# Paged cache loads of a hybrid S5 and MLA decoder step: two tokens to a partition on 64 partitions

## The chip, the cores and the metric

The kernel runs on one core of one Trainium2 chip. The metric is the device time of one execution in microseconds, the median over runs. All data are 32-bit floats.

## What is computed

One layer of a decoder, for a prompt of 512 tokens (with 16 learned meta tokens ahead of it) and for 8 samples that decode one token each. An input projection feeds an S5 state-space group and a latent attention group (MLA, 8 heads); both are gated, concatenated and projected back. What the change touches is the attention of the 8 samples over their cached past, 2048 tokens in 16 pages of 128 for each sample:

```python
def mla_sample_attn(q_abs, q_pe, c_new, kpe_new, c_pool, kpe_pool, page_table, w_uv):
    c_past = c_pool[page_table].reshape(dbs, -1, KV_LORA)        # KV_LORA = 512
    kpe_past = kpe_pool[page_table].reshape(dbs, -1, QK_ROPE)    # QK_ROPE = 64
    s_past = (jnp.einsum('bqhr,bkr->bhqk', q_abs, c_past)
              + jnp.einsum('bqhe,bke->bhqk', q_pe, kpe_past)) * SOFTMAX_SCALE
    ...
    w = jax.nn.softmax(jnp.concatenate([s_past, s_new], axis=-1), axis=-1)
    o_lat = (jnp.einsum('bhqk,bkr->bqhr', w[..., :n_past], c_past)
             + jnp.einsum('bhqk,bkr->bqhr', w[..., n_past:], c_new))
```

A page of cache_ckv is 128 x 512 floats (256 KB), one of cache_kpe 128 x 64 floats (32 KB). Which pages a sample has stands in a page table that is read at run time.

## The kernel before, in words

The program is written out engine by engine, with semaphores between them. Its stages in order of time are: normalising and transposing the input, the input projection, the S5 scan with its gate, the query, key and value projections, the attention of prompt and samples together, and the output projection with the final norm. The projections run on TensorE (PE) as three matmuls for each product, of high and low parts.

The attention stage is a loop over 32 steps n (`N_TILES`, four for each of 8 heads), unrolled on every engine. At each step the engines do one 128-query tile of the prompt's attention, and beside it one group of pages of a sample: 32 groups, four pages each, four groups for each sample.

- **Slots.** Seven slots (`RING`, line 412) hold a group each: `ckv[s]` is [128 partitions, 4, 512] and `kpe[s]` [128, 4, 64]; the second index j is the page of the group, and the partition is the token in the page.
- **Loads.** `load_pages` (lines 455 to 465) reads page numbers from the table into registers, waits until the slot's last user on PE is done (`opv_done`), and issues two DMAs for each page, one of cache_ckv (line 464) and one of cache_kpe (line 465). The first seven groups are loaded whole, one by SyncE's queue (SP, line 653) and six by GpSimd's (POOL, lines 814 to 826), ahead of the loop. Of each of the other 25 groups, SP loads pages 0 and 1 (lines 671 to 673) and POOL pages 2 and 3 (lines 827 and 828). On SP these loads stand in a written order between the loads of the prompt's heads: `hraw` (queries and keys, lines 618 to 625, of which line 624 loads rotary queries twice, once to partitions 0 to 63 and once to 64 to 127), `vraw` (line 629), `za` (line 633), and small stores to `u_d` (line 685).
- **Order.** `freed_at` (line 433) gives the step at which a slot is freed. Two groups are freed together, every two steps or so, so loads come in bursts of two groups. Each DMA adds 16 to a semaphore of its slot and queue; `loaded_counts` (line 450) gives the counts to wait for, 64 for each round of two pages on each queue.
- **Users.** VectorE (DVE) waits for a group (line 1790) and transposes it in 32 x 32 blocks, in two halves of two pages (`turn_pages`, line 1793), and its rotary keys (`turn_rotary`, line 1797). PE computes scores of two groups at once (`page_scores`, lines 2350 and 2354), DVE and ScalarE (ACT) do the maximum and the exponential, and at the steps of `freed_at` PE weighs the pages with their probabilities straight from `ckv[s][:, j, :]` (`weigh_pages`, line 2378), which frees the slot. The scores take keys as they come: each place (partition, j) of a group is one key, in ckv and in kpe alike.

Of the kernel before, what the change touches and what calls it, by code (L numbers as in the profile page):

```python
# [13 lines left out]
ds = bass.ds  # L14
# [49 lines left out]
def build(nc, d):  # L64
# [4 lines left out]
    def at(name, offset, shape, dt=F32):  # L69

        assert base + offset + math.prod(shape[1:]) * 4 <= 229344, name
        return nc.alloc_sbuf_tensor_at(name, shape, dt, offset=base + offset)

    with es:
        def sem(name):
            return es.enter_context(nc.semaphore(name))
# [102 lines left out]
        ckv = [at(f"ckv{i}", a, [P, 4, KV_LORA]) for i, a in enumerate(SLOT_AT)]  # L179
        kpe = [at(f"kpe{i}", a + 8192, [P, 4, QK_ROPE]) for i, a in enumerate(SLOT_AT)]  # L180
# [151 lines left out]
        page_loaded = [[sem(f"page_loaded_{q}{s}") for s in range(7)] for q in ("pool", "sp")]  # L332
# [96 lines left out]
        def pages_freed(i):  # L429

            return i + 1
# [23 lines left out]
        def load_pages(eng, i, halves, by_sync):  # L455

            pages = [eng.value_load(ptab[0:1, 4 * i + j:4 * i + j + 1], min_val=0, max_val=d["cache_ckv"].shape[1] - 1)
                     for half in halves for j in (2 * half, 2 * half + 1)]
            if i >= RING:
                eng.wait_ge(opv_done, pages_freed(i - RING))  # L460
            s = i % RING
            for at_j, page in enumerate(pages):
                half, j = halves[at_j // 2], 2 * halves[at_j // 2] + at_j % 2
                eng.dma_start(ckv[s][:, j, :], d["cache_ckv"][0, ds(page, 1)].rearrange("a k r -> (a k) r")).then_inc(page_loaded[by_sync][s], 16)  # L464
                eng.dma_start(kpe[s][:, j, :], d["cache_kpe"][0, ds(page, 1)].rearrange("a k r -> (a k) r")).then_inc(page_loaded[by_sync][s], 16)

        MX, NMS, SMS = 0, 8, 16

# [3 lines left out]
        def _(sp):  # L472
# [178 lines left out]
            sp.wait_ge(table_loaded, 16)  # L651
            sp.wait_ge(v_ready, 10)
            load_pages(sp, BY_SYNC, (0, 1), 1)
            for u in range(2):
                sp.wait_ge(v_stored[u], 16 * 5)
# [9 lines left out]
            for n in range(N_TILES):  # L665
                h = n // 4 + 1
                if n % 4 == 1 and h + 1 < N_HEADS:
                    sp.wait_ge(head_lo_done, h + 1)
                    load_raw(h + 1)
                    load_rotary(h + 1)  # L670
                for i in range(RING, N_GROUPS_OF_PAGES):
                    if freed_at(i - RING) == n:
                        load_pages(sp, i, (0,), 1)
                if n % 4 == 0 and n and h < N_HEADS:
                    sp.wait_ge(pv_done, h - 1)
                    load_v(h)
                    sp.wait_ge(o_gated, h - 1)
                    load_za(h)
                if n % 4 == 3 and 0 <= n // 4 - 1 < N_SAMPLE - 2:
                    s = n // 4 - 1  # L680
                    sp.wait_ge(o_copied, s + 1)
                    if s:
                        sp.wait_ge(rows_stored, 64 * s)
                    for j in range(4):
                        sp.dma_start(u_d[s * P + 32 * j:s * P + 32 * j + N_HEADS, 0:KV_LORA], osb[32 * j:32 * j + N_HEADS, s % 2, :]
                                     ).then_inc(rows_stored, 16)
# [50 lines left out]
        def _(pool):  # L737
# [76 lines left out]
            for i in (4, 5):  # L814
                load_pages(pool, i, (0, 1), 0)
# [1744 lines left out]
```

## Time and profile before

| | |
|---|---|
| median of 3 runs | 1157.97 us (1156.71 to 1161.84) |
| the profiled execution | 1155.58 us |
| its span | 1153.9 us |
| mean granted TensorE clock | 0.964 of full speed |
| PE busy | 1045.1 us, 91% |
| DVE busy | 609.7 us, 53% |
| ACT busy | 378.0 us, 33% |
| POOL busy | 170.6 us, 15% |
| bytes moved by DMA | 170.93 MB, 148 GB/s over the span |
| attention stage | about 723 to 928 us |

All durations below are from the one profiled execution. The times of an engine are busy times; its idle times are attributed to what released it. A DMA packet is a piece that one of the 16 DMA engines moves in one go; the share of a queue is the time its packets took, over 16 engines times the window. "Landing" is from the issue of a DMA to its completion.

### The profile page before, as it was taken

How to read it: one execution, taken by the hardware profiler on the slowest of the kernel's cores; microseconds unless marked ns; L12 is line 12 of the kernel's file. 1: busy time of each engine (PE TensorE's matmuls, PEld its weight loads, DVE VectorE, ACT ScalarE, POOL GpSimd, SP SyncE). 2: the span in 40 equal slices, each digit the busy share in tenths (PEclk: the TensorE clock that was granted, in tenths of full speed). 3: DMA queues.
4: the chain of work that ended last, by engine and by line, in shares of the span. 5: the costliest groups of instructions: out<-in, count | busy, mean ns of one | idle time of the engine just before them, and what ended most of it. 6: DMA issues, size and time to landing. Idle time of an engine off the chain costs nothing.

```text
span 1153.9 us, 26835 instructions
## 1 busy us (share of the span) xinstructions
PE 1045.1 (91%) x10642; PEld 964.7 (84%) x10642; DVE 609.7 (53%) x1253; ACT 378.0 (33%) x774; POOL 170.6 (15%) x257
## 2 busy tenths in 40 slices
PE   3899999999999999998899989678777789999995
PEld 2899999999999999997799977555545549999995
DVE  4366454451688821495765355767668542332432
ACT  6321112212233222154542222444545412332433
POOL 3002310000320000103504500123333100000000
PEclk9899999999999999999899989798999889999998
DMA  9446743223344443237456845567787786223213
GB/s 281 102 139 115 167 118 94 71 69 93 114 119 129 115 131 92 73 93 226 124 158 183 257 167 161 157 214 242 251 251 255 235 203 215 74 80 102 73 37 148
DMA packets 202059, 170.93 MB, mean 148 GB/s; under 512 B 37755, under 2 KB 166246, under 8 KB 200134
## 3 DMA queue, kind: packets, MB, share of 16 engines
q1 hardware_dynamic: 179078, 120.75, 37.5%
q0 software_dynamic: 11392, 28.52, 8.0%
q10 hardware_dynamic: 11496, 20.36, 4.8%
q8 instruction: 65, 1.06, 0.4%
q14 instruction: 28, 0.23, 0.1%
HBM read 141.93 MB, written 25.31 MB: 145 GB/s over the span
## 4 chain that ended last, share of the span: by engine, by line
PE 72%; DMA 9%; DVE 6%; issue 5%; ACT 4%; SPq 3%; POOLq 0%; ACTq 0%; POOL 0%; DVEq 0%
PE gemm L2065 12%; PE gemm L2066 12%; PE gemm L2067 12%; PE gemm L2420 5%; PE gemm L2422 5%; PE gemm L2421 5%; DMA kpe<-cache_kpe 4%; PE misc L2141 2%; PE misc L2336 2%; PE misc L2151 1%; PE misc L2092 1%; DMA w_raw<-w_glu 1%; DMA w_raw<-w_in 1%; PE gemm L2350 1%; DMA osr<-u_d 1%
## 5 line engine op out<-in xcount | busy, mean ns | idle before, releaser
L2065 PE MATMUL gemm<-xh,w_hi 128*128 128x260 f32 (+2 forms) x1056 | 302.3, 286 | 0.3 <-DVE w_lo L1333 0.3
L2066 PE MATMUL gemm<-xl,w_hi 128*128 128x260 f32 (+2 forms) x1056 | 300.7, 285 | 0.0
L2067 PE MATMUL gemm<-xh,w_lo 128*128 128x260 f32 (+2 forms) x1056 | 299.9, 284 | 0.0
L1333 DVE TENSOR_TENSOR w_lo<-w_raw,w_hi 128x2048 fp32r<-128x2048 f32 (+3 forms) x63 | 109.6, 1739 | 225.3 <-ACT w_hi L857 221.7
L857 ACT ACTIVATE w_hi<-w_raw 128x2048 fp32r<-128x2048 f32 (+3 forms) x63 | 90.7, 1439 | 337.2 <-PE gemm L2067 281.7
L2065 PEld LDWEIGHTS gemm<-xh,w_hi 128*128 128x128 f32 x1056 | 198.8, 188 | 1.2 <-DVE w_lo L1333 0.5
L2067 PEld LDWEIGHTS gemm<-xh,w_lo 128*128 128x128 f32 x1056 | 199.1, 189 | 0.0
L2066 PEld LDWEIGHTS gemm<-xl,w_hi 128*128 128x128 f32 x1056 | 198.9, 188 | 0.0
L2420 PE MATMUL gemm<-comb_hi,w_hi 128*128 128x260 f32 x512 | 147.7, 289 | 1.2 <-DVE comb_lo L1945 1.1
L2421 PE MATMUL gemm<-comb_lo,w_hi 128*128 128x260 f32 x512 | 145.3, 284 | 0.0
L2422 PE MATMUL gemm<-comb_hi,w_lo 128*128 128x260 f32 x512 | 145.3, 284 | 0.0
L2420 PEld LDWEIGHTS gemm<-comb_hi,w_hi 128*128 128x128 f32 x512 | 97.1, 190 | 4.0 <-issue 3.2
L2421 PEld LDWEIGHTS gemm<-comb_lo,w_hi 128*128 128x128 f32 x512 | 97.4, 190 | 0.0
L2422 PEld LDWEIGHTS gemm<-comb_hi,w_lo 128*128 128x128 f32 x512 | 97.3, 190 | 0.0
L1793 DVE STREAM_TRANSPOSE ct<-ckv 128x1024 f32<-128x1024 f32 x64 | 79.2, 1238 | 33.9 <-DMA kpe<-cache_kpe 33.6
L1934 DVE TENSOR_TENSOR yt<-yt,misc 128x512 f32 (+1 forms) x14 | 9.6, 687 | 98.5 <-PE misc L2481 98.5
L464 POOL DMA_DIRECT2D ckv<-cache_ckv x74 | 40.0, 541 | 144.1 <-PE gemm L2378 102.4
L1249 ACT ACTIVATE yb<-gemm 128x260 f32<-128x260 f32 x28 | 9.3, 385 | 106.2 <-PE gemm L2422 106.2
L1888 DVE TENSOR_TENSOR w_lo<-w_raw,w_hi 128x2048 fp32r<-128x2048 f32 x16 | 36.7, 2292 | 13.3 <-ACT w_hi L1237 13.2
L2164 PE MATMUL gemm<-ys_hi,w_hi 128*128 128x260 f32 x128 | 38.2, 298 | 5.1 <-DVE sig L1633 4.4
L2350 PE MATMUL gemm<-ct,qx 128*32 128x64 f32 x2048 | 38.9, 243 | 2.8 <-issue 2.8
L2065 PE MATMUL gemm<-qn_hi,w_hi 128*128 128x260 f32 x144 | 40.8, 283 | 0.5 <-DVE ev L1694 0.5
(383 smaller groups left out, 1990.2 us busy)
## 6 DMA issues: line engine op xcount, KB each, us to landing
w_raw<-w_in SPq DMA_DIRECT2D x35, 1024.0 KB, 6.3
ckv<-cache_ckv POOLq DMA_DIRECT2D x74, 256.0 KB, 4.3
w_raw<-w_out SPq DMA_DIRECT2D x16, 1024.0 KB, 5.8
ckv<-cache_ckv SPq DMA_DIRECT2D x54, 256.0 KB, 4.3
z_d<-ev ACTq DMA_DIRECT2D x16, 260.0 KB, 2.0
w_raw<-w_glu SPq DMA_DIRECT2D x8, 512.0 KB, 4.3
yt<-x_prompt SPq DMA_DIRECT2D x4, 1024.0 KB
o_y_p<-yt SPq DMA_DIRECT2D x4, 1024.0 KB
```

Of the source, the lines that this page charges most:

```text
L464: eng.dma_start(ckv[s][:, j, :], d["cache_ckv"][0, ds(page, 1)].rearrange("a k r -> (a k) r")).then_inc(page_loaded[by_sync][s], 16)
L857: act.activation(w_hi[:, slot, 0:width], w_raw[:, slot, 0:width], ACT.Copy).then_inc(w_hi_ready, 1)
L1333: dve.tensor_tensor(w_lo[:, slot, 0:width], w_raw[:, slot, 0:width], w_hi[:, slot, 0:width].bitcast(F32), ALU.subtract).then_inc(w_lo_read ...
L1793: dve.transpose(out=ct[:, n % 3, first:last].rearrange("p x r -> p (x r)"), in_=ckv[n % RING][:, first:last].rearrange("p x r -> p (x r)"))
L2065: pe.matmul(acc, a, xa, start=k == 0, stop=False)
L2066: pe.matmul(acc, a, xb, start=False, stop=False)
L2067: last = pe.matmul(acc, b, xa, start=False, stop=k == k_tiles - 1)
L2164: pe.matmul(acc, a, xa, start=k == 0, stop=False)
L2350: pe.matmul(SC[32 * j:32 * j + 32, c0:c0 + 64].rearrange("p (g t) -> p g t", g=2), qx[:, s % 2, r, :], ct[:, buffers, j, r * 32:(r + 1) * ...
L2420: pe.matmul(acc, a, comb_hi[:, k, c], start=k == 0, stop=False)
L2421: pe.matmul(acc, a, comb_lo[:, k, c], start=False, stop=False)
L2422: last = pe.matmul(acc, b, comb_hi[:, k, c], start=False, stop=k == KD - 1)
```

## The change

Each page goes to 64 partitions in place of 128, and each partition takes two consecutive tokens, which lie side by side in the pool and in the slot: 4096 contiguous bytes of cache_ckv and 512 of cache_kpe, where there were 2048 and 256. Pages 0 and 1 of a group share the columns j = 0 and 1 of the slot, page 0 on partitions 0 to 63 and page 1 on 64 to 127; pages 2 and 3 share j = 2 and 3 in the same way. The slots, semaphores, counts, queues and all that uses the pages stay as they are.

```diff
@@ -461,8 +461,11 @@
             s = i % RING
             for at_j, page in enumerate(pages):
                 half, j = halves[at_j // 2], 2 * halves[at_j // 2] + at_j % 2
-                eng.dma_start(ckv[s][:, j, :], d["cache_ckv"][0, ds(page, 1)].rearrange("a k r -> (a k) r")).then_inc(page_loaded[by_sync][s], 16)
-                eng.dma_start(kpe[s][:, j, :], d["cache_kpe"][0, ds(page, 1)].rearrange("a k r -> (a k) r")).then_inc(page_loaded[by_sync][s], 16)
+                rows, cols = slice(64 * (j % 2), 64 * (j % 2) + 64), slice(j - j % 2, j - j % 2 + 2)
+                eng.dma_start(ckv[s][rows, cols, :].rearrange("p t r -> p (t r)"), d["cache_ckv"][0, ds(page, 1)].rearrange("a (k t) r -> (a k) (t r)", t=2)
+                              ).then_inc(page_loaded[by_sync][s], 16)
+                eng.dma_start(kpe[s][rows, cols, :].rearrange("p t r -> p (t r)"), d["cache_kpe"][0, ds(page, 1)].rearrange("a (k t) r -> (a k) (t r)", t=2)
+                              ).then_inc(page_loaded[by_sync][s], 16)
 
         MX, NMS, SMS = 0, 8, 16
```

## Rows read from the trace of the kernel before

**Rows 1.** Chain of waits that ended last, 723 to 928 us: shares by line

```profile
by line: DMA kpe<-cache_kpe 22.3%; issue 15.7%; PE misc L2336 8.7%; PE gemm L2350 6.1%; PE gemm L2378 5.1%; DVE ct L1793 4.2%; SPq L465 3.6%; SPq L464 3.6%; PE misc L2315 2.7%; SPq L457 2.6%; SPq L624 2.0%; ACT prob L1170 1.7%; ACT hh L1067
```

**Rows 2.** List of waits, 715 to 935 us: total, times, longest

```profile
POOL ckv L464 <- PE gemm L2378: 102.4, 13, 27.7
...
DVE ct L1793 <- DMA kpe<-cache_kpe: 33.6, 18, 5.4
...
DVE mxt L1806 <- PE gemm L2354: 15.0, 6, 6.1
...
SPq L464 <- PE gemm L2378: 41.6, 8, 12.1
```

**Rows 3.** Timeline of SP's queue, one burst: start, duration

```profile
829.10 0.38 SPq L464 DMA_DIRECT2D ckv<-cache_ckv  x1
...
830.72 0.33 SPq L465 DMA_DIRECT2D kpe<-cache_kpe  x1
...
832.90 1.31 SPq L465 DMA_DIRECT2D kpe<-cache_kpe  x1
```

**Rows 4.** Timeline of POOL, the same burst

```profile
829.57 0.54 POOL L464 DMA_DIRECT2D ckv<-cache_ckv  x1 [10.00 <-PE gemm L2378]
...
831.62 0.54 POOL L465 DMA_DIRECT2D kpe<-cache_kpe  x1
```

**Rows 5.** Timeline of DVE, the same burst: idle time before, releaser

```profile
836.46 1.25 DVE L1793 STREAM_TRANSPOSE ct<-ckv 128x1024 f32<-128x1024 f32 x1 [1.86 <-DMA kpe<-cache_kpe]
```

**Rows 6.** Busy time by stretch; the last three: clock, DMA share, GB/s

```profile
820.00:845.00 25.00, 20.70 (x484) 14.43 (x476) 18.43 (x42) 11.45 (x35) 8.39 (x16) 0.98 0.78 249
```

**Rows 7.** DMA queues, 804 to 826 us (q1 is SP's, q0 POOL's)

```profile
DMA packets 4421, 6.18 MB, mean 281 GB/s; under 512 B 1680, under 2 KB 2208, under 8 KB 4416
...
q1 hardware_dynamic: 3520, 3.75, 56.6%
q0 software_dynamic: 896, 2.36, 31.8%
```

**Rows 8.** DMA queues, 739.0 to 739.5 us: 128 partitions, rows of 2 KB

```profile
q1 hardware_dynamic: 102, 0.19, 100.5%
```

**Rows 9.** DMA queues, 627 to 628 us (256 B), then 1000 to 1012 us (512 B)

```profile
q1 hardware_dynamic: 988, 0.25, 109.8%
...
q1 hardware_dynamic: 2064, 1.05, 31.1%
```

**Rows 10.** DMA queues, 740.1 to 740.7 us: two loads to 64 partitions each

```profile
DMA packets 110, 0.18 MB, mean 305 GB/s; under 512 B 21, under 2 KB 21, under 8 KB 110
...
q1 hardware_dynamic: 110, 0.18, 95.2%
```

**Rows 11.** Issue durations by line, ns: minimum, median, maximum, first and last start

```profile
L464 POOL DMA_DIRECT2D ckv<-cache_ckv x74: 537/537/709, 627.6 to 902.6; - x74
...
L464 SPq DMA_DIRECT2D ckv<-cache_ckv x54: 332/333/377, 722.6 to 902.1; - x54
...
L809 POOL DMA_DIRECT2D rp<-lat_d x2: 543/561/579, 626.5 to 627.1; - x2
...
L789 POOL DMA_DIRECT2D latq<-lat_d x1: 855/855/855, 522.4 to 522.4; - x1
...
L624 SPq DMA_DIRECT2D hraw<-qp_d x16: 458/550/1423, 702.8 to 863.2; - x16
```

**Rows 12.** DMA queues, 811 to 823 us, inside a burst

```profile
DMA packets 2787, 3.93 MB, mean 327 GB/s; under 512 B 869, under 2 KB 1397, under 8 KB 2785
```

**Rows 13.** Landing: the page's issues, 638 to 648 us, and cache_ckv's minimum

```profile
ckv<-cache_ckv POOLq DMA_DIRECT2D x74, 256.0 KB, 4.3
...
kpe<-cache_kpe SPq DMA_DIRECT2D x54, 32.0 KB, 5.0
...
ckv<-cache_ckv POOLq DMA_DIRECT2D x6, 256.0 KB, 3.3
...
DMA to landing us min/median/max: 2.5/4.3/6.6
```

## The prediction, made before the change was run

> **What bounds the kernel now.** I read the page first: PE is busy 91% of the span, and the paged attention is a stretch of about 205 us in the middle. Then I asked for the chain of waits over that stretch [rows 1]. The reader is to see that the largest share of it, 22.3% of 205 us or 45.7 us, is the flight of a page load, and that the rest is spread thin over PE, DVE, ACT and the queues. So here, unlike in the projections before and after, loads end waits. The list of waits says who waits [rows 2]: the DVE transposes of the pages lose 33.6 us in 18 waits to a cache_kpe load, which is the last DMA of a group on its queue. In the other direction POOL waits 102.4 us and SP 41.6 us until PE has weighed a group and its slot is free. That is the loop: PE frees a slot, both queues issue, the pages land, DVE transposes, PE scores and weighs.
>
> One turn of it in the timelines: SP issues its two pages of a group from 829.10 to 831.05 and has the next group under issue at 832.90 [rows 3]; POOL issues its two from 829.57 on, the last at 831.62 [rows 4]; DVE, which had to wait, starts on that group at 836.46 [rows 5]. So the group took 7.4 us from the first issue, of which 4.8 us lie after the last issue. Between 820 and 845 us the 16 DMA engines are busy 78% of the time at 249 GB/s, with the bursts near full and gaps between them [rows 6]. Both the throughput inside a burst and the latency at its end count.
>
> **What a page load costs in the DMA engines, and what the change makes of it.** A page is 262 KB of cache_ckv and 33 KB of cache_kpe. In the burst of 804 to 826 us SP and POOL load eight pages each. SP's queue shows 3520 packets, POOL's 896 [rows 7]. POOL's divide as 16 completions for each of 16 DMAs (256) and 640 data packets, 80 a page: with 2.36 MB that is 64 packets of 4 KB and 16 of 2 KB. So POOL's queue already joins two 2 KB rows into one packet. SP's are one for each contiguous row: of the 1680 packets under 512 B 256 are POOL's completions, and the other 1424 are 8 x 128 rows of cache_kpe and 400 completions of SP's.
>
> Prices of a packet, as the share of 16 engines times the window over the count:
> - 2 KB: 100.5% of 8 us over 102 packets is 79 ns [rows 8].
> - 256 B: 109.8% of 16 us over 988 is 17.8 ns; 512 B: 31.1% of 192 us over 2064 is 28.9 ns [rows 9].
> - A completion: in a window with 21 of them and 89 of 2 KB, 9.14 us less 89 x 79 ns leaves about 100 ns each [rows 10].
> - 4 KB: POOL's 31.8% of 352 us is 111.9 us; less 256 x 0.1 and 128 x 0.079 us there remain 76.2 us for 512 packets, 149 ns [rows 7].
>
> SP's page before: 128 x 79 ns + 128 x 17.8 ns = 10.1 + 2.3 = 12.4 us of engine time; after: 64 x 149 ns + 64 x 28.9 ns = 9.5 + 1.8 = 11.4 us. With 3.2 us for 32 completions, which stay, the saving is 1.0 of 15.6 us, that is 0.066 us of all 16 engines. POOL's page: the same 64 packets of 4 KB and, with four partitions of 512 B for an engine where there were eight of 256 B, the same 16 of 2 KB. Saving none.
>
> **Issue.** As many DMAs are issued as before: 54 + 54 on SP, 74 + 74 on POOL, with the same table reads before them. SP takes 333 ns for each, and POOL 537 ns [rows 11]. On POOL 64-row transfers took 561 ns, and one of 768 rows 855 ns, so halving the rows lies between -0.03 and +0.03 us for a DMA; I take 0. On SP the nearest 64-row row is 550 ns [rows 11], but that one has a strided source; the ends are 0 and +0.2 us for each of four DMAs of a group, and the first page's DMAs overlap with the flight, so +0.4 us for 18 waits, +7 us, is the upper end. I take 0, since a page's own source is contiguous. SP's occasional issue of 1.3 us (at 832.90 [rows 3]) is backpressure; half the descriptors may end it, which I leave at nothing to -1 us a period, about -6 us over the six periods of some 25 us, value 0: the engines are busy then.
>
> **Consumers.** The DVE transposes and PE's weighing read the same shapes of the same tiles; keys only change places, in ckv and kpe alike, and a softmax sum doesn't see their order. Counts of the semaphores stay (16 for each DMA), so no wait is added. So I cost them at nothing, and no cover is needed.
>
> **The sum.** A group holds two SP pages: -0.13 us. A burst is two groups, so its second group gains up to -0.26 us. Over 18 waits this is -2.4 to -4.7 us; I take -3. The profiled execution took 1155.6 us (span 1153.9) and so would give 1152.6; the median of the runs shown is 2.4 us above it, and on that scale I say 1155. The whole wait of 33.6 us is the lower end of what can be won, and it cannot be reached: the fastest landing of a page still takes 2.5 us [rows 13]. What is late next is PE's last score matmul, for which DVE waits 15 us in the stretch already [rows 2].
>
> **A place where row and rule part.** The two halves of the rotary queries are 64-partition loads on SP, one to partitions 0 to 63, then one to 64 to 127, just as this change does with pages. While they land, 740.1 to 740.7 us, the queue moves 305 GB/s, and with completions taken off, the packets cost what those of a 128-partition load cost [rows 8, 10]. By this row a half costs nothing, and it is why I take no penalty. It is 262 KB long, and partly both halves at once, so it does not exclude one. The Trainium skill ("SBUF — State Buffer", Door 1: The DMA port swizzle) speaks against the change: partitions 0 to 63 reach 8 of 16 ports, it gives 196 GB/s for 64 partitions and 328 for 128, and its next section says that two loads, one on each half, gain only 6%. Here 305 GB/s disagrees. By its asymptote of about 218 GB/s a page would take an estimated 1.35 us in place of 0.90, and if 18 waits pay that once, the time would be near 1166, if for all four pages, near 1190.
>
> **Rivals.**
> 1. Half the partitions, half the rate. Place: the start and the end of each burst, where one page of one queue flies alone, or all of it, if SP's and POOL's pages fall on the same half at the same time (both queues start with partitions 0 to 63). Price: at 327 GB/s, the rate of a burst [rows 12], a page of 295 KB takes 0.90 us, at half of it 1.80 us. One page for each of 18 waits: +16 us, 1174. All four pages of each: a period of 25 us, busy 19.5 us now, gets 16 x 0.9 = 14.4 us more, and so exceeds 25 us by 9; six periods make +54 us, 1212. For it: no row shows a transfer as long as a page to one half, from two queues at once. Against: rows 10; and POOL starts 0.5 us after SP, so that the queues may be on different halves. It decides as soon as an engine's 4 KB packet takes clearly over 149 ns. Slower than before.
> 2. The load's latency falls by more than its engine time. Landing takes 4.3 us (cache_ckv) and 5.0 (cache_kpe on SP) in the median, but 3.3 us in a stretch where POOL's loads are nearly alone [rows 13]. If SP's many small packets and its blocked issues make up this difference, 18 waits lose about 1 us each: -18 us, 1140. For it: POOL's packets, which are large, wait in the same engines as SP's 256 B ones, in turns. Against: the engine time saved is 6%.
> 3. The change does nothing: POOL's half of the pages sees the same packets, and on SP 2 KB packets run at nearly the rate of 4 KB ones (79 x 2 against 149 ns). Time 1158.
>
> **How the numbers follow.** Small gain, as summed: 0.42 (range 1150 to 1161). Rival 1: 0.25 for one page a wait, 0.10 for more. Rival 2: 0.20. Rival 3: 0.03. A measurement of this kernel tells about 0.5%, 5.8 us, from no change. Faster by over that: rival 2 and 0.09 of the first case, 0.29. Within: 0.33 + 0.03 = 0.36. Slower: 0.35. Cases of both signs hold most of the chance, so the range is wide: from 1143, which leaves out about half of rival 2, to 1179, which holds the lighter form of rival 1 and leaves out the heavy one.
>
> **What would show it.** Right: SP's queue shows 128 data packets a page in place of 256, POOL's keeps 80 data packets a page; 4 KB packets near 149 ns on both; DVE's wait for cache_kpe falls to about 30 us; DVE, PE and issue durations unchanged. Rival 1: packet time well over 149 ns, the rate in a burst under 300 GB/s, DVE's wait over 45 us, DMA share in the stretch towards 1. Rival 2: landing near 3.5 us and the wait near 15. The forecast is wrong if that wait moves by more than 6 us either way.

## The result and the profile after

| | before | after |
|---|---|---|
| median of the runs, us | 1157.34 (4 runs, 1154.73 to 1161.84) | 1215.89 (4 runs, 1211.19 to 1217.57) |
| ratio after to before, 95% interval | | 1.0482 [1.0453, 1.0512] |
| span of the profiled execution, us | 1153.9 | 1212.5 |
| mean granted clock | 0.964 | 0.944 |

The change costs 58 us. The prediction, 1155 in a range of 1143 to 1179, is wrong.

Where the time went, first by stretches of the kernel after: length, busy time of PE, weight load, DVE, ACT and POOL, then clock, DMA share and GB/s.

```profile
600.00:720.00 120.00, 109.39 (x767) 100.69 (x766) 55.86 (x99) 26.69 (x41) 29.91 (x49) 0.94 0.66 174
720.00:985.00 265.00, 182.13 (x3274) 121.78 (x3276) 148.35 (x322) 99.94 (x293) 58.39 (x109) 0.84 0.80 183
985.00:1212.00 227.00, 208.45 (x1745) 198.26 (x1737) 73.10 (x114) 69.20 (x208) 0.65 (x1) 0.95 0.40 117
```

The same stretches of the kernel before:

```profile
600.00:720.00 120.00, 115.20 (x828) 104.37 (x827) 59.93 (x106) 30.72 (x45) 30.41 (x49) 0.97 0.61 190
720.00:928.00 208.00, 160.19 (x3239) 107.93 (x3241) 145.13 (x316) 97.29 (x289) 60.60 (x109) 0.90 0.73 227
928.00:1153.00 225.00, 207.27 (x1733) 197.98 (x1725) 72.06 (x114) 68.73 (x207) 0.00 (x0) 0.96 0.40 117
```

The last stretch, after the attention, is as long as before (227 against 225 us). The attention has the same work (DVE 148 against 145 us busy) in 265 us in place of 208. The DMA engines are busier (0.80 against 0.73) and move less (183 against 227 GB/s). So each byte costs more engine time; there is no lack of requests. Already from 600 to 720 us, when POOL loads the first pages beside weights, the rate falls from 190 to 174 GB/s, and PE is busy 5.8 us less in that stretch. PE's granted clock falls in the attention from 0.90 to 0.84 of full speed, and less in the stretches around it (0.97 to 0.94 and 0.96 to 0.95). PE waits more there; I read the fall as a consequence of the waits, which no run isolates. For the same matmuls PE is busy 182 in place of 160 us. Most of that is not on the chain of waits below: PE's lines there hold some 42 us, where they held 46.

The waits of the kernel after, 715 to 990 us (total, times, longest), answer to [rows 2]:

```profile
POOL ckv L465 <- PE gemm L2381: 131.9, 12, 30.2
DVE ct L1796 <- DMA kpe<-cache_kpe: 81.1, 20, 8.7
...
DVE mxt L1809 <- PE gemm L2357: 14.0, 4, 6.4
```

DVE's wait for a page has grown from 33.6 us in 18 to 81.1 us in 20: +47.5 us, beside a loss of 58. What was named as late next, the wait for PE's score matmul, has hardly moved. The chain that ended last, 723 to 985 us, by line, and its longest pieces (start, us), answers to [rows 1]:

```profile
by line: DMA kpe<-cache_kpe 32.7%; issue 14.9%; SPq L465 5.9%; PE gemm L2381 5.2%; SPq L467 4.7%; PE misc L2339 4.7%; PE gemm L2353 4.3%; SPq L457 2.7%; SPq L633 2.4%; PE misc L2318 1.7%; SPq L627 1.6%; DVE ct L1796 1.5%; POOLq L74 1.0%; SP
...
777.33 13.15 DMA kpe<-cache_kpe
...
810.02 12.43 DMA kpe<-cache_kpe
...
842.19 12.63 DMA kpe<-cache_kpe
...
874.24 13.14 DMA kpe<-cache_kpe
...
907.14 13.64 DMA kpe<-cache_kpe
```

By these shares the flights of pages on the chain hold 85.7 us (32.7% of 262) where they held 45.7, and SP's page issues 27.8 where they held 14.8. Once a period of the attention (32.4 us, four groups) there is one flight of 12.4 to 13.6 us. It belongs to the first group that SP issues behind the loads of the prompt's next head, as its timeline shows for the third of them (842.19):

```profile
837.65 1.11 SPq L627 DMA_DIRECT2D hraw<-qp_d  x2
...
842.19 0.47 SPq L467 DMA_DIRECT2D kpe<-cache_kpe  x1
```

The packets of that group wait behind those of the head's loads on SP's queue: by the packet records it moves mostly the head's rows from 840 to 845 us, and the pages' 4 KB packets from there to 855. POOL's pages share the engines from 843 on. Before, this place had the longest flight too, and it was shorter:

```profile
866.75 8.93 DMA kpe<-cache_kpe
```

The period, start to start of those flights, is 32.4 us (777.33 to 907.14 in four), where the prediction worked with 25. Five such periods at +7.4 us make 37 us, and the rest of the 58 lies at the edges of the attention. Some 8 us of it are lost before the loop has begun: SP issues its first page at 730.3 us in place of 722.6.

The queues, 750 to 990 us, which hold 50 of POOL's pages in either kernel (packets, MB, share of 16 engines): before, then after.

```profile
q1 hardware_dynamic: 37534, 38.74, 54.5%
q0 software_dynamic: 5600, 14.75, 18.5%
```

```profile
q1 hardware_dynamic: 20739, 28.92, 51.1%
q0 software_dynamic: 5600, 14.75, 28.0%
```

POOL's queue moves the same bytes in the same number of packets, 112 a page with completions, for half as much engine time again: 18.5% of 3840 us over 50 pages was 14.2 us a page, 28.0% is 21.5. In the trace's packet records of the same window (size and duration of each packet), POOL's 3200 packets of 4 KB rise from 193 to 291 ns in the mean (medians 162 and 302). In the microsecond from 798 to 799 POOL's page flies alone:

```profile
DMA packets 63, 0.22 MB, mean 221 GB/s; under 512 B 9, under 2 KB 9, under 8 KB 63
...
q0 software_dynamic: 54, 0.22, 104.7%
q1 hardware_dynamic: 9, 0.00, 1.0%
```

104.7% of 16 us over 54 packets is 310 ns for 4 KB, and the rate is 221 GB/s with all engines busy. The nine other packets are completions, and they took 0.16 us together, 18 ns each. In the packet records before, a completion takes 9 to 10 ns. The prediction had priced it at about 100, and so had put too much of POOL's time down to completions: its 149 ns for a packet of 4 KB [rows 7] were 191 in that burst, with the median at 169. The count of packets came out as predicted. Their price rose to one and a half times in the mean, and to about twice the median of before when a page flies alone. Landing and issues answer to [rows 13] and [rows 11]:

```profile
ckv<-cache_ckv POOLq DMA_DIRECT2D x74, 256.0 KB, 7.3
...
ckv<-cache_ckv SPq DMA_DIRECT2D x54, 256.0 KB, 7.9
```

```profile
L465 POOL DMA_DIRECT2D ckv<-cache_ckv x74: 516/521/531, 625.8 to 958.2; - x74
...
L465 SPq DMA_DIRECT2D ckv<-cache_ckv x54: 468/469/1333, 730.3 to 957.9; - x54
```

A page lands in 7.3 us where it took 4.3. Besides, SP needs 469 ns for an issue in place of 333. That is a second candidate.

### The profile page after: what moved, and what is told of

Same layout as the page of the kernel before. It is cut to its first block, busy times and chain, and to the rows that moved or that the text cites. A ratio compares the mean times of both kernels' runs of the same rounds, so it can differ in the third digit from the quotient of the medians.

```text
span 1212.5 us, 26835 instructions
## 1 busy us (share of the span) xinstructions
PE 1062.9 (88%) x10642; PEld 975.8 (80%) x10642; DVE 607.4 (50%) x1253; ACT 377.9 (31%) x774; POOL 168.3 (14%) x257
## 2 busy tenths in 40 slices
DMA packets 195147, 170.93 MB, mean 141 GB/s; under 512 B 30843, under 2 KB 162790, under 8 KB 193222
## 4 chain that ended last, share of the span: by engine, by line
PE 68%; DMA 12%; DVE 5%; SPq 5%; issue 5%; ACT 3%; POOLq 0%; ACTq 0%; DVEq 0%; POOL 0%
PE gemm L2068 12%; PE gemm L2069 11%; PE gemm L2070 11%; DMA kpe<-cache_kpe 7%; PE gemm L2423 5%; PE gemm L2425 5%; PE gemm L2424 5%; DMA w_raw<-w_uk 2%; PE misc L2144 2%; SPq L465 1%; PE misc L2154 1%; PE gemm L2381 1%; PE misc L2095 1%; DMA w_raw<-w_glu 1%; DMA w_raw<-w_in 1%
## 5 line engine op out<-in xcount | busy, mean ns | idle before, releaser
L1796 DVE STREAM_TRANSPOSE ct<-ckv 128x1024 f32<-128x1024 f32 x64 | 79.2, 1238 | 81.4 <-DMA kpe<-cache_kpe 81.1
L2353 PEld LDWEIGHTS gemm<-ct,qx 128*32 128x32 f32 x2048 | 37.5, 131 | 7.1 <-issue 6.7
```

The lines of the kernel that those rows point to most:

```text
L1796: dve.transpose(out=ct[:, n % 3, first:last].rearrange("p x r -> p (x r)"), in_=ckv[n % RING][:, first:last].rearrange("p x r -> p (x r)"))
L2353: pe.matmul(SC[32 * j:32 * j + 32, c0:c0 + 64].rearrange("p (g t) -> p g t", g=2), qx[:, s % 2, r, :], ct[:, buffers, j, r * 32:(r + 1) * ...
```

## The experiments

The main theory: the 64 contiguous partitions are the cause; what goes into one half of the partitions is limited to about 210 GB/s. Against this theory stood the long packet itself, both queues on the same half at the same time, SP's dearer issue, and engines that reach one half slowly. The diffs are against the changed kernel where nothing else is said.

**Every second partition in place of a half.** Same packets, same 64 rows, other partitions.

```diff
-                rows, cols = slice(64 * (j % 2), 64 * (j % 2) + 64), slice(j - j % 2, j - j % 2 + 2)
+                rows, cols = slice(j % 2, P, 2), slice(j - j % 2, j - j % 2 + 2)
```

> A page still goes to 64 partitions with two tokens each, but to every second partition of the 128 (page j on partitions j mod 2, j mod 2 + 2, ...) in place of one half. Theory 1, the half: what the changed kernel lost, it lost because the 64 partitions of a page lie in one half of the SBUF, into which only some 220 GB/s go (its bursts run flat at 200 to 240 GB/s, before 270 to 370). Then this layout is as fast as before or a little faster, 1150 to 1158 us, bursts at 300 GB/s or more, 4 KB packets near 149 ns. Theory 2, the long packet: 4 KB written into a single partition take 310 ns in place of two times 79. Then this one is as slow as the changed kernel, 1210 to 1220 us, with packets near 310 ns. Theory 3, the queue: an issue on SP takes 469 ns in place of 333 with this access pattern, four times a group; then nothing changes against the changed kernel either, 1216 us, at whatever rate of the bursts.

Measured: 1165.51 against 1159.97 us, ratio 1.0059 [1.0035, 1.0082], a little slower than the 1150 to 1158 that the theory gave. Landing of cache_ckv (POOL, then SP, as in all that follows) is 4.4 and 4.3 us, DVE's wait 42.6 us in 16. POOL's pages are back at the old engine time (750 to 990 us), and inside a burst, 798 to 802 us, the rate is that of before or more:

```profile
q0 software_dynamic: 5600, 14.75, 18.6%
```

```profile
DMA packets 708, 1.48 MB, mean 370 GB/s; under 512 B 163, under 2 KB 351, under 8 KB 708
```

One line brings the loss from 4.82% to 0.59%, with the long packets left in. The cause of most of it is which partitions the rows go to.

**The half without the long packet.** 64 contiguous partitions, but rows of 2 KB: tokens k and k + 64 share a partition.

```diff
-                eng.dma_start(ckv[s][rows, cols, :].rearrange("p t r -> p (t r)"), d["cache_ckv"][0, ds(page, 1)].rearrange("a (k t) r -> (a k) (t r)", t=2)
+                eng.dma_start(ckv[s][rows, cols, :], d["cache_ckv"][0, ds(page, 1)].rearrange("a (t k) r -> (a k) t r", t=2)
...
```

> The changed kernel with 2 KB packets: page j on the same 64 partitions of one half, but token k and token k + 64 of the page go to partition k, so every run of contiguous bytes is one token (2048 bytes of cache_ckv, 256 of cache_kpe). Theory 1, the half: as slow as the changed kernel, 1205 to 1225 us, bursts at 200 to 240 GB/s. Theory 2, the long packet: back near the kernel before, 1150 to 1165 us. Theory 3, the queue: depends on the issue time that the profile then shows; at 469 ns like the changed kernel 1216 us, at 333 ns 1157 us.

Measured: 1217.87 against 1159.97 us, 1.05 [1.0468, 1.0533]; landing 7.0 and 7.5 us. The half costs all of it even with rows of 2 KB. SP's page packets are of 2 KB here; POOL's are as many as before (5600 in the window), so its queue still joins two rows, and only their destination is split. Issues are dearer still (604 ns on POOL, 605 on SP), and that too hardly shows.

**Opposite halves on the two queues.** SP begins with partitions 0 to 63 and POOL with 64 to 127.

```diff
-                rows, cols = slice(64 * (j % 2), 64 * (j % 2) + 64), slice(j - j % 2, j - j % 2 + 2)
+                side = (j + j // 2) % 2
+                rows, cols = slice(64 * side, 64 * side + 64), slice(j - j % 2, j - j % 2 + 2)
```

> The changed kernel, but pages 2 and 3 of a group, which POOL loads, change halves: page 2 goes to partitions 64 to 127, page 3 to 0 to 63. SP still begins with 0 to 63. So at any time the two queues tend to fill different halves. Theory 1, the half: most of the loss comes back, since both halves fill at once: 1155 to 1180 us, bursts mostly over 280 GB/s. Theory 2, the long packet, and theory 3, the queue: no change against the changed kernel, 1210 to 1220 us.

Measured: 1211.04 us, 1.0451 [1.0422, 1.048]; landing 7.0 and 7.0 us, DVE's wait 68.9 us in 20. A miss: I had expected most of the loss to go. The two queues being on one half together is not the main thing.

**A quarter for each page.** Page j lies on partitions 32j to 32j + 31, in rows of 8 KB.

```diff
-                rows, cols = slice(64 * (j % 2), 64 * (j % 2) + 64), slice(j - j % 2, j - j % 2 + 2)
+                rows = slice(32 * j, 32 * j + 32)
...
+                eng.dma_start(ckv[s][rows, :, :].rearrange("p t r -> p (t r)"), d["cache_ckv"][0, ds(page, 1)].rearrange("a (k t) r -> (a k) (t r)", t=4)
...
```

> Each page goes to 32 partitions with four tokens each (8192 contiguous bytes of cache_ckv): page j on partitions 32 j to 32 j + 31. SP's pages 0 and 1 both lie in the first half, POOL's 2 and 3 both in the second. Theory 1, the half: each queue has a half of its own, some 220 GB/s each, together up to 440, if a quarter takes as much as a half: 1150 to 1170 us. If instead the rate goes with the number of partitions of a page, 32 are half as fast again, and it is slower than the changed kernel: over 1260 us. Theory 2, the long packet: packets of 8 KB into one partition take 620 ns, and it stays at 1210 to 1220 us or above.

Measured: 1213.13 us, 1.0469 [1.0447, 1.0491]; landing 7.7 and 6.7 us. A miss as well: SP's pages now lie in the lower half and POOL's in the upper, throughout, and it is no better than the change. SP's issue fell to 316 ns here, so with an issue as cheap as in the kernel before the loss stays.

**Every fourth partition.** As the quarters, but spread, again 8 KB rows. The diff is against the quarters.

```diff
-                rows = slice(32 * j, 32 * j + 32)
+                rows = slice(j, P, 4)
```

> Each page on 32 partitions with four tokens each, but on every fourth of the 128 (page j on j, j + 4, ...), so packets are 8 KB as in the quarters kernel (1213 us) and the partitions spread as in the every-second kernel (1165.5 us against 1160). Theory 1, spread: what counts is how a page's partitions lie over the SBUF, and it is as fast as before or faster, 1148 to 1162 us; its issues on SP should take about 320 ns as those of the quarters, and if the 0.6% of the every-second kernel came from its 469 ns, that is gone here. Theory 2, packets of 8 KB or few rows cost: 1200 us or more.

Measured: 1165.94 against 1161.58 us, 1.0045 [1.0019, 1.0072]; landing 4.2 us on both, DVE's wait 38.4 us. SP's issue is 473 ns, where I had expected about 320, and the time is above the expected 1148 to 1162. Beside the quarters this is the cleanest pair: same rows, same 8 KB, +0.45% spread and +4.69% contiguous, although the spread one has the dearer issue.

**Only one queue's pages changed.** First the two pages of a group that SP mostly loads (pages 0 and 1, of which POOL loads 12), then the other two (`j >= 2`), which are POOL's but for two.

```diff
...
+                if j < 2:
+                    rows, cols = slice(64 * (j % 2), 64 * (j % 2) + 64), slice(j - j % 2, j - j % 2 + 2)
...
+                else:
+                    eng.dma_start(ckv[s][:, j, :], d["cache_ckv"][0, ds(page, 1)].rearrange("a k r -> (a k) r")).then_inc(page_loaded[by_sync][s], 16)
...
```

> Only pages 0 and 1 of a group, SP's, go to 64 partitions with two tokens each; pages 2 and 3, POOL's, are loaded as before. If the loss goes with the engine time of the pages (POOL's 14.2 us a page before, 21.5 after), half of it remains: 1180 to 1195 us. If the issue time of SP's DMAs had a large part in it, most of it: over 1200.

> The reverse: only pages 2 and 3, POOL's, go to half the partitions, and SP's are as before. By engine time half of the loss, 1180 to 1195 us. If the issue time of SP was a large part, clearly less than the kernel with only SP's pages changed: 1165 to 1180 us.

Measured against 1161.58 us: pages 0 and 1, 1194.99 us, 1.031 [1.0262, 1.0357], landing 5.8 and 6.3 us; pages 2 and 3, 1202.42 us, 1.0374 [1.0327, 1.0421], landing 6.2 us on both. The second is slower than the 1180 to 1195 that I had expected. SP issues its own pages there in 333 ns as before, and still it costs 41 us. Pages of the untouched queue land late too (SP's in 6.2 us for 4.3): the engines are shared, and a slow packet of one queue holds up the other's. +33 and +41 us together are more than the +58 of both; they are not additive, which would fit a loop where the later of two loads decides, but no run shows that.

**SP's issue time alone.** The kernel before, with one more read of a page number after each of SP's pages. The read is of no use.

```diff
+                if by_sync:
+                    eng.value_load(ptab[0:1, 4 * i:4 * i + 1], min_val=0, max_val=d["cache_ckv"].shape[1] - 1)
```

> The kernel before with one more read of the page table on SP after each of its pages, whose result nothing uses: some 0.45 us of SP's time a page, 0.9 a group. The two layouts that spread a page over all partitions (every second, every fourth) ended 0.6% and 0.45% above the kernel before although their pages land no later (4.1 to 4.4 us against 4.2 to 4.5); their DMAs take 470 ns to issue on SP in place of 333, 0.56 us a group. If SP's longer issues are the cause, this kernel loses about 1.6 times as much, 4 to 12 us: 1164 to 1172. If not, and the rest comes from the longer packets, it stays within 2 us of the kernel before.

Measured: 1168.22 against 1159.21 us, 1.0062 [1.0037, 1.0088]; DVE's wait 45.3 us. SP's timeline of the kernel before and of this one (start, duration), from the first page's last issue to the second page's first:

```profile
829.66 0.37 SPq L465 DMA_DIRECT2D kpe<-cache_kpe  x1
830.21 0.33 SPq L464 DMA_DIRECT2D ckv<-cache_ckv  x1
...
835.25 0.37 SPq L465 DMA_DIRECT2D kpe<-cache_kpe  x1
836.38 0.57 SPq L464 DMA_DIRECT2D ckv<-cache_ckv  x1
```

1.13 us from start to start, where 0.55 us stood before: a read is 0.58 us, two a group 1.16 us, for +9.0 us. The change adds 4 x 0.136 = 0.54 us a group to SP's queue, by the same slope an estimated +4.2 us. The spread layouts, which have the same dear issue, lose 5.5 and 4.4 us, so their remaining loss would be explained by it; no run has a spread layout with a cheap issue. Of the 58 us of the change, this second term is an estimate and not isolated: the quarters, with 316 ns, lose 4.69% [4.47, 4.91], and the half with rows of 2 KB, with 605 ns, 5.0% [4.68, 5.33], and both intervals overlap the change's [4.53, 5.12].

**Page numbers ahead of the wait.** If time on the queues counts, take some away: layout of the kernel before, but the numbers of both groups of a burst are read before the wait for the slot.

```diff
...
+        def load_freed(eng, n, halves, by_sync):
+            groups = [i for i in range(RING, N_GROUPS_OF_PAGES) if freed_at(i - RING) == n]
+            numbers = [read_pages(eng, i, halves) for i in groups]
+            for i, pages in zip(groups, numbers):
+                load_pages(eng, i, halves, by_sync, pages)
...
```

> The layout of the kernel before, but where two groups are freed together, each queue reads the page numbers of both ahead of its wait, in place of the second two numbers between the two groups' DMAs. That gap is 1.15 us on SP and 1.17 us on POOL in the kernel before. If time on SP's queue in a burst is worth what the kernel with added reads lost (0.9 us a group cost 7 us over 25 groups), this gains up to 1.15 us for each of 12 second groups, 2 to 8 us: 1151 to 1158. If the second group of a burst is bound by what the DMA engines still have to move, it gains nothing: within 2 us of the kernel before.

Measured: 1161.76 against 1156.88 us, 1.0043 [1.0015, 1.0072]: slower, where I expected it faster. DVE's wait is as before (34.0 us). Why it is slower stays open, and so the slope of the run above is no general price of SP's time. None of the versions beats the kernel before.

**The same kernel.** Two blank lines added to the kernel before, to see what difference shows where there is none.

```diff
+
+
```

> The kernel before with two blank lines added and nothing else. It shows what the comparison gives for no change: four kernels that should have been near the kernel before ended 0.43% to 0.62% above it, one of which was expected below. If the ratio here is within 0.2% of 1, those differences are theirs; if it is 1.004 or more, a kernel's own build or place in the run adds as much, and they mean nothing.

Measured: 1161.04 against 1159.23 us, 1.0003 [0.9978, 1.0028]. The four differences of 0.4 to 0.6% (every second, every fourth, the added read, the numbers ahead) have intervals that begin at 1.0015 or above, and this one holds 1. They are small; a single such kernel does not show that another build could not differ by as much.

**Loads alone.** A program that leaves the whole computation out, writes zeros, and loads pieces of the cache into one tile, in fifteen stages, each waited for. SP issues, in two stages ACT too. This program and the next ran once each. The entries are (first partition, step, rows, floats of a row):

```diff
+    ("S", [(0, 1, 128, 512)] * 8),
+    ("S", [(0, 1, 64, 1024)] * 8),
+    ("S", [(64, 1, 64, 1024)] * 8),
+    ("S", [(0, 1, 64, 1024), (64, 1, 64, 1024)] * 4),
+    ("S", [(0, 2, 64, 1024), (1, 2, 64, 1024)] * 4),
+    ("SA", [(0, 1, 64, 1024), (64, 1, 64, 1024)] * 4),
+    ("SA", [(0, 1, 64, 1024), (0, 1, 64, 1024)] * 4),
...
+    ("S", [(0, 4, 8, 4096)] * 4),
+    ("S", [(64, 4, 8, 4096)] * 4),
+    ("S", [(0, 1, 8, 4096)] * 4),
+    ("S", [(0, 1, 4, 4096)] * 4),
+    ("S", [(0, 8, 16, 4096)] * 4),
...
```

> Leaves the whole computation out: loads only, in 15 stages, each begun when the one before has landed, outputs are zeros. A stage is eight loads of 256 KB (the last six: four loads of rows of 16 KB). 1: 128 partitions. 2: partitions 0 to 63. 3: 64 to 127. 4: these halves in turns. 5: every second partition. 6: SP into 0 to 63 and ACT into 64 to 127 at once. 7: both into 0 to 63. 8: partitions 0 to 31. 9: every fourth of the 128. 10: 8 rows to 0, 4 .. 28. 11: 8 rows to 64, 68 .. 92. 12: 8 rows to 0 to 7. 13: 4 rows to 0 to 3. 14: 16 rows to 0, 8 .. 120. 15: 16 rows to 0 to 15. Theory A, a limit on what goes into a half at a time: stages 2, 3, 8 at 220 GB/s or less, 1, 5, 9 at 350 to 430, stage 6 also at 350 or more, 7 at 220. Theory B, each of the 16 DMA engines reaches one half fast and the other slowly, whatever the others do: 2, 3, 4, 6, 7 and 8 all alike, and stages 10 and 11, which have 8 rows for 8 engines, differ from each other by half or more. Theory C, groups of four partitions have a limit of 27 GB/s each, as TensorE's 128 partitions of 2 KB give 430/16: 10 and 11 alike at up to 218, 12 at 54, 13 at 27, 15 at 109 GB/s.

The rates inside a stage, in this order: 128 partitions (6 to 8 us), 0 to 63 (12.5 to 19.5), 64 to 127 (25 to 31.5), the halves in turns (36.5 to 43), every second (50 to 53), one half by SP and the other by ACT (57.5 to 62.5), both on the lower half (68.5 to 75), 0 to 31 (80 to 87):

```profile
DMA packets 433, 0.79 MB, mean 395 GB/s; under 512 B 47, under 2 KB 47, under 8 KB 433
...
DMA packets 448, 1.45 MB, mean 207 GB/s; under 512 B 94, under 2 KB 94, under 8 KB 448
...
DMA packets 414, 1.34 MB, mean 207 GB/s; under 512 B 86, under 2 KB 86, under 8 KB 414
...
DMA packets 464, 1.52 MB, mean 234 GB/s; under 512 B 92, under 2 KB 92, under 8 KB 464
...
DMA packets 333, 1.10 MB, mean 367 GB/s; under 512 B 64, under 2 KB 64, under 8 KB 333
...
DMA packets 379, 1.25 MB, mean 251 GB/s; under 512 B 73, under 2 KB 73, under 8 KB 379
...
DMA packets 410, 1.37 MB, mean 211 GB/s; under 512 B 76, under 2 KB 76, under 8 KB 410
...
DMA packets 264, 1.44 MB, mean 206 GB/s; under 512 B 88, under 2 KB 88, under 8 KB 88
```

207 GB/s into either half, 367 with the same rows spread. The two halves in turns, which is what the change does on each queue, give 234, and two queues on opposite halves 251, no doubling, where theory A had 350 or more. In the packet records a packet of 4 KB takes 320 ns on a half and 170 with the rows spread.

The stages with few rows of 16 KB show the unit of the limit. Rows to partitions 0, 4, ... 28 (99 to 105 us), to 64, 68, ... 92 (105.5 to 111), to 0 to 7 (110.5 to 119), to 0 to 3 (119.5 to 130), and 16 rows to 0, 8, ... 120 (133.5 to 140.5):

```profile
q1 hardware_dynamic: 64, 0.52, 27.0%
...
q1 hardware_dynamic: 64, 0.52, 28.7%
...
q1 hardware_dynamic: 56, 0.52, 50.5%
...
q1 hardware_dynamic: 35, 0.26, 20.0%
...
q1 hardware_dynamic: 128, 1.05, 67.4%
```

27.0% of 16 x 6 us is 25.9 us for 32 rows, 0.81 us a row, and 28.7% of 16 x 5.5 us is 0.79 us: an engine reaches either half equally well, which rules out theory B, engines that are slow towards one half. On four neighbours a row takes 2.1 us (20.0% of 168 us over 16 rows), and eight rows to two such fours take 2.1 us as well. These are means; in the packet records the middle row of both takes 2.40 us, and rows that had fewer beside them are faster. Four rows on their way at once, 66 KB in 2.40 us, are 27 GB/s. And 16 rows to 0, 8, ... 120, each in a four of its own, take 1.18 us (median 1.27), more than 0.81. There every row shares something with one other; if that is the partition 32 further, 33 KB in 1.27 us are 26 GB/s. (Completions are in these shares; at 9 to 35 ns each they change nothing.) So the limit is as theory C has it, one of the destination, and fits entrances of about 27 GB/s, each for four partitions and the four 32 further on. A half has eight of them, an estimated 8 x 27 = 216 GB/s, near the 207 measured. The pairing with p + 32 rests on that stage and on partitions 0 to 31, which have just as many such fours as 0 to 63 if they are paired, and reached the same rate (206 against 207 GB/s).

The Trainium skill ("SBUF — State Buffer", section "Door 1: The DMA port swizzle") has just this map, with 16 ports of eight partitions, and 196 GB/s measured for partitions 0 to 63; the runs agree (207).

**Loads alone, second program.** Also without the computation. It asks whether the length of the run matters, and when opposite halves help.

```diff
+    ("S", [(0, 1, 128, 512)] * 8),
+    ("S", [(0, 2, 64, 1024)] * 8),
+    ("S", [(0, 2, 64, 4096)] * 4),
+    ("S", [(0, 1, 64, 4096)] * 4),
...
+    ("SA", [(0, 1, 64, 1024), (64, 1, 64, 1024), (64, 1, 64, 1024), (0, 1, 64, 1024)] * 3),
+    ("SA", [(0, 1, 64, 1024), (0, 1, 64, 1024), (64, 1, 64, 1024), (64, 1, 64, 1024)] * 3),
+    ("SA", [(0, 1, 64, 1024), (64, 1, 64, 1024)] * 6),
...
```

> Leaves the whole computation out, like the first kernel of loads: 12 stages, one after another. It asks why two queues that fill opposite halves at once reached only some 260 GB/s, though the halves together have the ports of the whole. Theory K: each DMA engine works through its packets in order, all 16 in step, and two engines meet at the same group of four partitions (0 to 63: engine e and e + 8; every second partition: e and e + 4); what they lose depends on how long they stay on one group before they change to another. Theory L: the number of halves in flight counts, not the order. Stages: 1: 128 partitions, rows of 2 KB: 380 GB/s or more. 2: every second partition, 4 KB: 360 or more. 3: every second, 16 KB, so that an engine stays on a group for 32 KB where it was 8: by K down to 220 to 280, by L 380 or more. 4: partitions 0 to 63, 16 KB: 215. 5: 128 partitions, 16 KB: 420. 6: even partitions on SP beside odd ones on ACT: 360 or more. 7: half 0 on SP beside half 1 on ACT with rows of 1 KB: by K more than the 260 of rows of 4 KB, unless the issues limit it. 8: the same, both half 0: 215 or less. 9: 4 KB, the queues on opposite halves, each changing half from load to load: 230 to 280 by K. 10: both on the same half, changing together: 210 to 235. 11: half 0 on SP and half 1 on ACT throughout, 12 loads: 260. 12: every fourth partition, 16 KB: by K 220 to 280.

Every second partition with rows of 4 KB (11 to 16 us) and of 16 KB (20 to 29), the half with 16 KB (33 to 53); then two queues, on even and on odd partitions (77.5 to 81.5), on opposite halves that both change in turn (102 to 112), together on one half that changes (117 to 127), and one half each throughout, early (132.5 to 135.5) and late (138.5 to 142):

```profile
DMA packets 504, 1.67 MB, mean 333 GB/s; under 512 B 97, under 2 KB 97, under 8 KB 504
...
DMA packets 273, 3.69 MB, mean 410 GB/s; under 512 B 48, under 2 KB 48, under 8 KB 48
...
DMA packets 293, 3.75 MB, mean 188 GB/s; under 512 B 64, under 2 KB 64, under 8 KB 64
...
DMA packets 452, 1.52 MB, mean 380 GB/s; under 512 B 81, under 2 KB 81, under 8 KB 452
...
DMA packets 755, 2.50 MB, mean 250 GB/s; under 512 B 144, under 2 KB 144, under 8 KB 755
...
DMA packets 692, 2.28 MB, mean 228 GB/s; under 512 B 135, under 2 KB 135, under 8 KB 692
...
DMA packets 209, 0.70 MB, mean 232 GB/s; under 512 B 39, under 2 KB 39, under 8 KB 209
...
DMA packets 308, 1.01 MB, mean 289 GB/s; under 512 B 62, under 2 KB 62, under 8 KB 307
```

Theory K, that engines in step make the spread layout slow with 16 KB rows, does not hold: 410 GB/s, and every fourth partition with 16 KB gave 325, where it had 220 to 280. Two queues do add up to the full rate where both are spread (380 GB/s). Opposite halves reach 232 to 289 GB/s, rising over 9 us in the one stage that keeps to them, and a burst of the kernel has hardly longer. This agrees with the two misses above. Two stages with rows of 1 KB moved 126 GB/s and tell nothing of the halves. Why two halves together don't give twice 207 GB/s stays open.

## Why the prediction was wrong

- **What bounds the kernel: right.** The loads' flight was the largest part of the chain, and most of the loss is there: +40 us of flight on the chain, +47.5 us of DVE's wait, of +58 us.
- **Counts of packets: right.** SP's pages went to 128 data packets. The packets under 512 B of the whole execution fell from 37755 to 30843, by 6912 = 54 x 128. POOL's stayed at 112 with completions.
- **Price of a packet: the step that failed.** "By this row a half costs nothing, and it is why I take no penalty" took the 4 KB price over from 128-partition loads, 149 ns; measured are 310 ns alone and 291 in the mean, where the kernel before has 193. The comparison of [rows 10] with [rows 8] was circular: the completions' 100 ns had been worked out by giving the half's packets the price of the 128-partition load. With completions at the 9 ns of the packet records, the larger packets cost 100 ns in [rows 10] and 88 in [rows 8], whose 102 packets hold 12 completions. So the row did show a penalty, a small one. It did not show the limit: 262 KB, the two halves one right behind the other, 305 GB/s; loads to the halves in turns, with rows of 4 KB and repeated, gave 234 in the first load program. What lets the short pair run faster was not tried. I had written that the row did not exclude a penalty, and still set it to zero.
- **The saving on SP's queue:** by the prediction's own prices it is 0.063 us for a page and not 0.066. It is too small to be seen beside the rest, and no run shows it.
- **Issue of SP: mis-sized.** Taken as 0 with +0.2 us a DMA as the upper end; measured +0.136 us, worth an estimated 4.2 us by the delay experiment, and not isolated in the changed kernel. That page rows are contiguous in memory did not make them cheap. POOL's issues even fell, 537 to 521 ns, as bounded. Half the descriptors did not end SP's occasional long issues: the longest of a cache_kpe load is 1.55 us, where it was 1.34.
- **Rival 1: the right mechanism, in its heavy form,** which had 0.10 and lay outside the range. Its decision point held (4 KB clearly over 149 ns, and over the 193 that a packet really took before), and so did two of its marks: under 300 GB/s in a burst (208 from 804 to 826 us, where it was 281) and DVE's wait over 45 us. The third did not: the DMA share went from 0.73 to 0.80 and not towards 1. The size, +54 us to 1212, was near by luck, with a wrong working. It had packets at exactly double and periods of 25 us grown by 9; measured are +7.4 us in periods of 32.4, with 21.5 in place of 14.2 us of engine time for a POOL page, and POOL's early pages slow before the attention begins.
- **"POOL starts 0.5 us after SP, so that the queues may be on different halves"** counted against rival 1. By the run with opposite halves it is worth little: 1211.04 us.
- **The place where rule and row part:** the rule on one half held. By the Trainium skill ("SBUF — State Buffer", Door 1) 218 GB/s is the asymptote of one half; 221 GB/s is measured over the one microsecond with POOL's page alone, and 207 over longer stretches of the load program. Its section "Can I just issue two DMAs to hit both halves?" gives 6%. Measured are 13% for one queue in turns (234 against 207) and 19% for two queues (251 against 211): more, but no way out. The mistake in my use of it was to charge each wait with the longer time of its own pages only, and to leave out that all 16 engines are held for that time, so that the other queue's loads and the head's loads take longer too; "if for all four pages, near 1190" was 26 us low.
- **Rival 2** (latency falls with fewer small packets): next to nothing of it. With SP's packets halved in number and the rows spread, cache_ckv landed in 4.2 to 4.4 us against 4.3. SP's cache_kpe, for which DVE waits, landed in 4.4 to 4.5 against 5.0, half a microsecond and not one, and DVE's wait did not fall (38.4 and 42.6 us against 33.6). **Rival 3** is out.
- **Consumers: right.** DVE's 64 page transposes take 1238 ns each, as before.

## What to carry to other kernels

Choose a load's destination partitions before its packet size: 64 neighbours took about 207 GB/s where every second partition took 367 with the same rows, and a slow load also holds up every other queue, since the engines are shared. If a tile wants several tokens to a partition, deal the loads out with a stride (page j on partitions j, j + 4, ...) and not in blocks; where a load can take all 128 partitions, as here, no layout did better. A short transfer of the trace is no proof that a layout is free; where a row and a rule part, measure or price both, and price the slower one for all transfers that share the engines.

## What the runs showed of the hardware that I had not expected

- Two queues on opposite halves do not add up: 251 GB/s against 211 on the same half, and in the other load program 232 rising to 289 over 9 us. On even and odd partitions they reach 380.
- The completion of a DMA on an engine is a packet of 4 bytes and takes 9 to 10 ns in the kernel before, not the 100 that the prediction had.
- With the partitions spread, rows of 2, 4 or 8 KB land equally fast: 4.3 us before, then 4.3 and 4.2. In the contiguous layouts it is 7.5, 7.9 and 6.7 (all cache_ckv on SP; on POOL 7.0, 7.3 and 7.7).
- An issue of SP depends on the destination: for cache_ckv 333 ns with 128 partitions, 469 with 64 neighbours, 474 with every second, 473 with every fourth, but 316 with 32 neighbours.
- Two reads of a page number a group, 1.16 us of SP's queue, cost 9 us in all, although SP waits 41.6 us for free slots in the same stretch [rows 2]. Two such reads moved ahead of the wait gained nothing (+0.43%), unexplained.
